# Gated-DeltaNet block on one core: first-level mask put on the decays beforehand, value scaling and output norm moved ahead, convolution steps spread over the levels

## The reference, cut to what matters

```python
gc = jnp.cumsum(g, axis=-1)
decay = jnp.exp(jnp.where(causal, gc[..., :, None] - gc[..., None, :], -jnp.inf))
A = jnp.where(strict, jnp.einsum('bhnid,bhnjd->bhnij', k * beta[..., None], k) * decay, 0.0)
T = lax.linalg.triangular_solve(eye + A, eye, left_side=True, lower=True)
u = T @ (v * beta[..., None])
w = T @ (k * beta[..., None] * jnp.exp(gc)[..., None])
attn_qk = jnp.einsum('bhnid,bhnjd->bhnij', q * dk ** -0.5, k) * decay
...
v_new = u_n - w_n @ state
o = q_dec @ state + attn_qk @ v_new
state = state * jnp.exp(g_last) + k_dec.T @ v_new
...
o = rms_norm(o, gdn_norm_g) * jax.nn.silu(z)
y = sc_b * causal_depthwise_conv(sc_c * sc_h, conv_sc_w)   # 3 taps, then a norm per group
```

## Time and profile before

| | |
|---|---|
| median of 3 runs | 3408.28 us (3407.03 to 3412.93) |
| profiled execution, its own time | 3409.73 us |
| span of its trace | 3408.0 us |
| PE busy | 3201.0 us, 94% of the span |
| DVE, ACT, POOL busy | 35%, 28%, 29% |
| mean granted TensorE clock | 0.977 of 2.4 GHz |

### The profile page before, as it was taken

How to read it: one execution, slowest core, us unless ns; L and a number is a source line. 1 busy time by engine, 2 the same in 40 slices (tenths; PEclk the granted TensorE clock), 3 DMA queues, 4 the chain that set the end, 5 groups by cost and what they waited for, 6 DMA issues and landing times.

```text
span 3408.0 us, 41850 instructions
## 1 busy us (share of the span) xinstructions
PE 3201.0 (94%) x14862; PEld 2599.3 (76%) x14862; DVE 1186.8 (35%) x1554; ACT 963.2 (28%) x1721; POOL 982.3 (29%) x806
## 2 busy tenths in 40 slices
PE   6898999899989999999979989998999999999998
PEld 5686777677768888888858767776776788888887
DVE  0554555452241121122146445544433321121113
ACT  3422444232231111111142234442412311111112
POOL 5222333322112332332322233324211232332332
PEclk9899999999999999999979999999999999999999
DMA  3322121311101111111132222214111011111111
GB/s 129 124 90 96 58 75 62 126 50 47 43 25 50 49 62 37 49 49 49 43 131 84 101 72 72 64 34 158 44 43 43 25 62 37 49 55 43 49 48 69
DMA packets 106110, 221.52 MB, mean 65 GB/s; under 512 B 8928, under 2 KB 52000, under 8 KB 105888
## 3 DMA queue, kind: packets, MB, share of 16 engines
q1 hardware_dynamic: 45536, 157.90, 13.8%
q10 hardware_dynamic: 60480, 62.44, 5.4%
HBM read 185.67 MB, written 34.64 MB: 65 GB/s over the span
## 4 chain that ended last, share of the span: by engine, by line
issue 52%; PE 25%; POOL 15%; DVE 3%; ACT 2%; DMA 2%; POOLq 1%; DVEq 0%; SPq 0%; ACTq 0%
POOL w_lo L1467 10%; PE PS L1809 5%; PE PS L1811 5%; PE PS L1810 5%; POOL row_lo L369 3%; PE PS L1160 2%; PE PS L1182 1%; PE PS L1140 1%; DMA raw<-in_w_units 1%; PE PS L1172 1%; PE PS L1213 1%; PE PS L1203 1%; PE PS L1194 0%; ACT w_hi L1525 0%; DMA qkvz_d<-stage 0%
## 5 line engine op out<-in xcount | busy, mean ns | idle before, releaser
L1809 PE MATMUL PS<-act_hi,w_hi 128*128 128x512 f32 (+1 forms) x2624 | 1053.6, 402 | 18.0 <-ACT stage L415 7.1
L1811 PE MATMUL PS<-act_hi,w_lo 128*128 128x512 f32 (+1 forms) x2624 | 1023.1, 390 | 0.0
L1810 PE MATMUL PS<-act_lo,w_hi 128*128 128x512 f32 (+1 forms) x2624 | 1022.7, 390 | 0.0
L1467 POOL TENSOR_TENSOR w_lo<-raw,w_hi 128x1024 fp32r<-128x1024 f32 x252 | 607.0, 2425 | 895.1 <-ACT w_hi L1525 894.5
L1809 PEld LDWEIGHTS PS<-act_hi,w_hi 128*128 128x128 f32 x2624 | 498.5, 190 | 117.8 <-issue 23.2
L1811 PEld LDWEIGHTS PS<-act_hi,w_lo 128*128 128x128 f32 x2624 | 497.1, 189 | 103.0
L1810 PEld LDWEIGHTS PS<-act_lo,w_hi 128*128 128x128 f32 x2624 | 498.6, 190 | 94.9 <-issue 2.9
L1722 DVE TENSOR_TENSOR h<-h,PS 128x1024 f32<-128x1024 f32 x304 | 371.2, 1221 | 429.6 <-PE PS L1846 428.4
L1842 PE MATMUL PS<-w_hi,row_hi 128*128 128x512 f32 x1088 | 428.9, 394 | 5.6 <-DVE row_lo L1067 5.6
L1846 PE MATMUL PS<-w_hi,row_lo 128*128 128x512 f32 x1088 | 424.8, 390 | 0.0
L1844 PE MATMUL PS<-w_lo,row_hi 128*128 128x512 f32 x1088 | 424.8, 390 | 0.0
(11 more groups left out here) (230 smaller groups left out, 2930.7 us busy)
## 6 DMA issues: line engine op xcount, KB each, us to landing
raw<-in_w_units SPq DMA_DIRECT2D x252, 512.0 KB, 3.3
h<-in_x SPq DMA_DIRECT2D x16, 1024.0 KB, 8.8
qkvz_d<-stage ACTq DMA_DIRECT2D x64, 256.0 KB, 2.6
qk<-qkvz_d ACTq DMA_DIRECT2D x32, 256.0 KB, 2.8
out<-result ACTq DMA_DIRECT2D x16, 512.0 KB, 4.3
xn<-mix_d ACTq DMA_DIRECT2D x12, 512.0 KB, 4.3
vv<-qkvz_d ACTq DMA_DIRECT2D x16, 256.0 KB, 4.2
zz<-qkvz_d ACTq DMA_DIRECT2D x16, 256.0 KB, 3.5
```

Source lines behind the costliest of these rows:

```text
L1467: pool.tensor_tensor(w_lo[slot][:, :], raw[raw_slot][:, :], w_hi[slot][:, :].bitcast(f32), ALU.subtract)\
L1809: nc.tensor.matmul(out_ap, whi, xhi, start=start, stop=False)
L1810: nc.tensor.matmul(out_ap, whi, xlo, start=False, stop=False)
L1811: return nc.tensor.matmul(out_ap, wlo, xhi, start=False, stop=stop)
```

## The change

- POOL's `decays_pool` gets a third product between its two: decays (already times beta) times `first_mask`, into `am0`. DVE then makes `am0` directly from the products in PSUM, ahead of A instead of behind it; it needs POOL's three products where it needed two.
- On DVE, `normalise_o` of the chunk before and `vb` move from behind `Xm` to the front of the `gram` step.
- On ACT, `rms_estimate` goes ahead of `sc_rms`, and `ln_norms` of the next chunk goes ahead of the `sc_u` copy and the `w_hi` of step `y6`.
- On DVE, the six taps move from `y3, y4, y5` to `x1, x3, x4` (one each), `x5` (two) and `x6` (one, followed by the halo copy).

```diff
@@ decays_pool (POOL)
             pool.tensor_tensor(dec[par][:, 0, :, :], dec[par][:, 0, :, :], gate("beta", m),
                                ALU.mult).then_inc(S["decm_ready"], 1)
+            pool.wait_ge(S["decm_ready"], n * 3 + 1)
+            pool.wait_ge(S["a1t_full"], n)
+            pool.tensor_tensor(am0[:, :, :], dec[par][:, 0, :, :], over_heads(first_mask[:, :]),
+                               ALU.mult).then_inc(S["decm_ready"], 1)
             pool.tensor_tensor(dec[par][:, 1, :, :], dec[par][:, 1, :, :], over_heads(upto[:, :]),
                                ALU.mult).then_inc(S["decm_ready"], 1)
@@ chunk_act (ACT)
                 if step == "gram":
                     if not first:
+                        rms_estimate(act, n - 1)
                         if par == 0:
                             sc_rms(act, R - 1, 0)
-                        rms_estimate(act, n - 1)
...
+                if step == "y6" and not last:
+                    ln_norms(act, n + 1)
                 if par == 0 and step == "y2":
...
-                if step == "y6" and not last:
-                    ln_norms(act, n + 1)
@@ chunk_dve (DVE)
                 if step == "gram":
 
+                    if not first:
+                        normalise_o(dve, n - 1)
+                    dve.wait_ge(S["vn_full"], n)
+                    dve.wait_ge(S["vt_full"], n + 1)
+                    dve.tensor_tensor(vb[:, :, :], r4(bank(3)), gate("beta", m), ALU.mult)\
+                        .then_inc(S["vb_ready"], 1)
                     dve.wait_ge(S["gram_full"], n + 1)
-                    dve.wait_ge(S["decm_ready"], n * 2 + 2)
+                    dve.wait_ge(S["decm_ready"], n * 3 + 3)
+                    dve.tensor_tensor(two(am0[:, :, :]), gram[:, :, :, 0, :], two(am0[:, :, :]),
+                                      ALU.mult).then_inc(S["am0_ready"], 1)
                     dve.tensor_tensor(two(A[:, 0, :, :]), gram[:, :, :, 0, :], two(A[:, 0, :, :]),
                                       ALU.mult).then_inc(S["a_ready"], 1)
-                    dve.wait_ge(S["a_ready"], n + 1)
-                    dve.tensor_tensor(am0[:, :, :], A[:, 0, :, :], over_heads(first_mask[:, :]),
-                                      ALU.mult).then_inc(S["am0_ready"], 1)
                 if step == "a1t":
 
                     dve.wait_ge(S["a1t_full"], n + 1)
-                    dve.wait_ge(S["vn_full"], n)
...
-                    dve.wait_ge(S["vt_full"], n + 1)
-                    dve.tensor_tensor(vb[:, :, :], r4(bank(3)), gate("beta", m), ALU.mult)\
-                        .then_inc(S["vb_ready"], 1)
...
                 if step == "y1":
-                    if not first:
-                        normalise_o(dve, n - 1)
...
-                if par == 1 and step in ("y3", "y4", "y5"):
-                    for i, c in {"y3": ((0, 0), (1, 0)), "y4": ((2, 0), (0, 1)),
-                                 "y5": ((1, 1), (2, 1))}[step]:
-                        sc_tap(dve, R, j, c, i)
-                if par == 1 and step == "y6":
+                if par == 1 and step in ("x1", "x3", "x4"):
+                    sc_tap(dve, R, j, 0, {"x1": 0, "x3": 1, "x4": 2}[step])
+                if par == 1 and step == "x5":
+                    sc_tap(dve, R, j, 1, 0)
+                    sc_tap(dve, R, j, 1, 1)
+                if par == 1 and step == "x6":
+                    sc_tap(dve, R, j, 1, 2)
                     dve.tensor_copy(sc_halo[:, bass.ds(j, 1), :].rearrange("p n k -> p (n k)"),
                                     sc_u[:, HALF:HALF + 2]).then_inc(S["sc_halo_out"], 1)
```

## The result

The changed kernel takes 3388.2 us (median of 4 runs, 3385.95 to 3392.05); the kernel before, on the same chip, 3409.2 (4 runs, 3407.03 to 3412.93). The ratio is 0.9939, 95% interval 0.9921 to 0.9956: faster by 0.6%, 21 us. The forecast was 3413.4, no change on its slow side, and the range began at 3400. It was wrong in sign and missed the range.

What follows compares the result with a forecast made beforehand. PE was taken to set the pace in most levels, DVE having room. Terms -1.4 - 2.4 - 1.8 + 10.7 = +5.1 on an execution of 3409.73 gave 3414.8, less 1.4 to the median: 3413.4 us, range 3400 to 3419.

Steps and rivals of the forecast that it cites:

- Part 4: End of an even chunk: late `w_lo` delays `kqn` and `ge`, PE's first state product waits for `ge`; +10.7 us.
- the collision: End of an even chunk: POOL's products get in between DVE's `kqn` and `ge` operations; +1.45 us in six chunks.
- no collision: Rival, even chunk's end: `kqn` or `ge` precedes POOL, or `w_lo` isn't late; -4.5 there, 3398.2 us in all; chance 0.16.
- Part 1: Start of a chunk, 14 times: `am0` 0.40 later, but PE's next product 0.10 earlier as `vb` is done; -1.4 us.
- +2.05: Start of a chunk: time in us from PE's `am0` transposes, through two pieces of fill, to its next product.
- Part 2: Taps in odd chunks: one moves from ahead of level 5's `Xm`, PE comes 0.40 earlier six times; -2.4 us.
- Part 3: First chunk of a half: half of PE's 1.89 wait for `vb` is won, given POOL's third product; -1.8 us.
- the front loses: Rival, start of a chunk: later `am0` isn't won back, +5.6 in place of -1.4; 3420.4 us in all; chance 0.14.

Runs made afterwards that it cites:

- e7_o_waits: The changed kernel with one added wait, PE's first state product in even chunks waiting for the `ge` made in the same chunk: 3409.70 us, ratio 1.0002 to the kernel before.
- e3_vb: The kernel before with `vb` alone moved to the front of the `gram` step: 3398.48 us against 3409.75, ratio 0.9963.
- e4_norm: The kernel before with the output norm alone moved to the front of `gram` and `rms_estimate` ahead of `sc_rms`: 3411.39 us against 3409.75, ratio 1.0005.
- e10_all: The changed kernel with the norm's large product behind `Xe`, `am0` ahead of `vb`, `x3` tap at `x2`, even-chunk `wt` ahead of `exp_norms`: 3368.22 us, 0.9880 of kernel before.

## Why the prediction was wrong

**Part 4 is the step that failed.** The sentence is "PE's first state product ... would now start at 520.6, waiting for `ge`: +1.45". All that stands ahead of it in that part came true: `ln_norms` first, `w_lo` late, `kqn` 2.02, POOL's products one by one in between, `ge` late. But `normalise(dve, n + 1, 1 - par)` makes the `ge` of the next chunk, and PE waits for `qdec_ready` at n + 1, a count reached one chunk earlier. I never asked which `ge` `o` reads; the description ahead of the prediction makes the same mistake. The rows couldn't tell: in the earlier trace rows `ge` ended at 517.79 and `o` started at 519.11, and in every other chunk of that trace that makes one `ge` was over, too, more than a microsecond ahead of `o`. Only the count in the code says it. Of what the collision delays, only `kqn` is needed soon, at the next `gram` step, and at 515.34 it is there in time. The part gave 6 x -0.47 in the even chunks and -0.9 in each first chunk, -4.6 us: the "no collision" value of -4.5, with the collision. The forecast had this gain right as well (0.45 left at `v`, since `wt` comes no earlier). The move alone measured -5.1. And the wait put in (`e7_o_waits`) lost 21 us.

**Part 1 had the right mechanism and the wrong size.** -0.10 a chunk was forecast, with -0.27 as its best case; it was -0.64 in odd and -0.74 in even chunks, 8 x -0.64 + 6 x -0.74 = -9.6 against -1.4. gram to a1t rose by 0.38 and 0.34 (0.40 forecast). Two terms are missing behind it; a third, small one is x1 to y2, 0.07 shorter, whose cause I haven't looked for.

- An idle time on PE can be longer than it is drawn. The earlier trace rows has 0.50 ahead of y1, but a1t to y1 fell by 0.67. The fill products start 0.23 apart and each is drawn 0.40 long, so the last one's drawn end covers 0.17 us in which PE would have gone on. That is why the forecast's "+2.05" from a1t to y1 was really 1.88.
- A whole wait was hidden in the same way. The code says `if l == 1: pe.wait_ge(S["on_ready"], n)`, so `x1` needs the output norm. In the kernel before:

```profile
452.97 0.40 PE L1811 MATMUL PS<-act_hi,w_lo 128*128 128x512 f32 x1
...
453.46 0.68 PE L1182 MATMUL PS<-Ym,Tm 128*128 128x128 f32 x4
```

The next product was due at 453.20 and is drawn from 453.46, 0.15 behind the end of `osq` (452.62 + 0.69); as the row ahead of it ends at 453.37, the profile shows no wait at all. Moved ahead, the norm gives back 0.28 (odd) and 0.34 (even). `e3_vb` made the wait visible, and `e4_norm` took it away alone. The Trainium skill (Perfetto Trace Analysis, section "Identifying the Most-Contended Engine") says that the busy share of the matmul track is not a good measure of how close a kernel is to the roofline, because pipelined instructions look smaller in the trace. In these rows each product is drawn longer than its spacing (0.40 against 0.23), and the overlap hides short waits; how far the kernel is from the roofline no run here shows.

What the Trainium skill (VectorE: DVE Perf Modes, section "The DRAIN you can't avoid") would have added to part 1 did not come: `osq`, `vb` and `am0` start 0.61 and 0.60 apart where each takes 0.68 to 0.69, also at the new place. The section itself adds that a next operation that is not held starts earlier; the rows agree with that.

**Part 2 was right**: x4 to y5 -0.40 in three odd chunks a half, -2.4; alone it measured -3.6, interval -6.8 to -1.0.

**Part 3 was right in kind**, and half of its 1.89 was about right. What waits there now is DVE for POOL's third product (1.78), as forecast, and from gram to y3 the two first chunks won 0.78 and 0.61: -1.4 against -1.8. The forecast had no term for the clock there, and that it needed none is luck. From a1t to y3 these chunks took 9.97 and 9.85 us at a mean clock of 0.83 before, and 9.11 and 9.06 at 0.81 after; but in the two halves of `e10_all` the same stretch took 10.32 at 0.67 and 8.31 at 1.00. So the clock of one execution can outweigh this part.

Together -9.6 - 2.4 - 1.4 - 4.6 = -18.0, the -18.0 read off the recurrences. Of the forecast's error of 25 us, part 4 made 15.3 and part 1 8.2. The rival "no collision" (3398.2) had the right sum for part 4 for a wrong reason; "the front loses" was wrong by the two missing terms. The sentence "I am wrong if PE doesn't wait for `ge` there" was the one to watch.

What stays open: the 3 to 4 us by which the whole exceeds -18.0. In the traces they lie outside the recurrences, and most of them in the clock: its length times the missing share of the granted clock comes to 74.0 us there before and to 70.8 after. Whether the change has a part in them is not shown. In the traces of all runs the time outside the recurrences (first `gram` step to last state product of each half) is 2785.8 to 2788.2 us without the whole change (5 kernels) and 2783.5 to 2788.9 with all or most of it (7 kernels).

## What to carry to other kernels

Before a late buffer is priced, find the count that its reader waits for, and which turn of the loop produced it: with two buffers in turn a name in a row doesn't tell which one is read. Read PE's waits from start to start against the spacing of undisturbed products, and list every wait in the code ahead of an instruction, since a wait shorter than the drawn overlap shows no idle time. And ahead of a wait for PE, put only what the next product needs; of what is needed later, the small steps may go in the gap and the large product behind.

## What the runs showed of the hardware

- DVE and POOL took turns when both had operations on SBUF queued without a wait: in the rows above DVE's three products (2.02, 1.52, 1.64 long, `ge` alone 0.69 in the earlier trace rows) and POOL's three (1.33, 1.60, 1.72, alone 1.04 in the earlier trace rows) alternate. Each is drawn from before the end of the other engine's; DVE's end 0.54 to 0.55 behind the end of POOL's, POOL's 0.9 to 1.1 behind the end of DVE's. The Trainium skill (SBUF — State Buffer, section "Who interferes with whom") says that a DVE instruction with two SBUF inputs contends with a GpSimd instruction that reads SBUF, and that the port pair they share is an exclusive lock. The rows agree, and add that neither engine got two turns in a row.
- An idle time of 2.0 us on PE (`e7_o_waits`), in a stretch at full clock, was followed by a clock of 0.50 (1.2 GHz) for some 3 us in two of eight places, and by nothing in the other six.
- In the first chunk of a half PE has two idle times close together (1.68 and 0.97 in the changed kernel). Of the 24 such chunks in the twelve traces, the clock behind them fell to 0.50 for some 3.4 us in 17 and for some 6.8 us in 3, and stayed full in 4.
